# Expert 0 of a hybrid decoder layer: its rows picked by products with a slot matrix instead of gathered

## The reference

```
x = x + mix @ w_out                       # residual rows
h = rmsnorm(x, g_ffn)                     # x * 1/std(x) * g_ffn
logits = h @ w_router + b_router          # 512 x 32
top_val, top_idx = top_k(logits, 4); gates = softmax(top_val)
# for each expert e, on the rows of the tokens that chose it:
hu = h_rows @ w1[e] + b1[e]               # 1024 -> 2048
act = clamped_swiglu(hu)
y = act @ w2[e] + b2[e]                   # 1024 -> 1024
x = x + sum over the 4 experts of gate * y
out = rmsnorm(x, g_final)
```

## Time and profile before

| | us |
|---|---|
| median of 3 runs | 1236.43 (1236.21 to 1237.57) |
| the profiled execution | 1236.09 |
| its span, from first to last instruction | 1234.5 |
| PE busy, share of the span | 1158.3 (94%) |
| DVE busy | 306.6 (25%) |
| ACT busy | 191.7 (16%) |
| POOL busy | 174.2 (14%) |
| read from HBM | 442.60 MB |

### The profile page before, as it was taken

How to read it: one execution, slowest core, us unless ns; L and a number is a source line. 1 busy time by engine, 2 the same in 40 slices (tenths; PEclk the granted TensorE clock), 3 DMA queues, 4 the chain that set the end, 5 groups by cost and what they waited for, 6 DMA issues and landing times. The chain is left out here.

```text
span 1234.5 us, 16405 instructions
## 1 busy us (share of the span) xinstructions
PE 1158.3 (94%) x7022; PEld 481.7 (39%) x7022; DVE 306.6 (25%) x484; ACT 191.7 (16%) x378; POOL 174.2 (14%) x250
## 2 busy tenths in 40 slices
PE   5999998799999999999999999999999999999980
PEld 4777787223333333333333333333333333333330
DVE  4677756421111010101101010110101011010117
ACT  4453422011100101001100000110000010100002
POOL 6000100432101111110111111111111111111000
PEclk9999998799999999999999999999999999999996
DMA  9400675599999999999999999999999999999996
GB/s 336 148 1 3 224 309 214 173 368 404 426 426 425 426 429 423 426 425 429 424 425 425 427 427 424 427 426 427 423 426 427 426 425 427 426 425 427 427 383 235
DMA packets 51147, 454.39 MB, mean 368 GB/s; under 512 B 13044, under 2 KB 13316, under 8 KB 26400
## 3 DMA queue, kind: packets, MB, share of 16 engines
q1 hardware_dynamic: 42864, 434.16, 84.7%
q0 software_dynamic: 7632, 17.05, 3.6%
q10 hardware_dynamic: 576, 2.10, 0.4%
HBM read 442.60 MB, written 15.12 MB: 371 GB/s over the span
## 5 line engine op out<-in xcount | busy, mean ns | idle before, releaser
L846 PE MATMUL ps<-ring_a,blockT 128*64 128x512 f32 x1472 | 326.6, 597 | 8.5 <-DMA ring_a<-in_w 8.5
L1307 DVE TENSOR_SCALAR xnT<-ps 128x768 f32<-128x768 f32 (+1 forms) x32 | 26.9, 841 | 814.8 <-PE ps L853 516.1
L846 PEld LDWEIGHTS ps<-ring_a,blockT 128*64 128x64 f32 x1472 | 102.4, 137 | 218.5 <-issue 199.9
L872 PE MATMUL ps<-ring_a,actT 128*64 128x512 f32 x736 | 165.3, 596 | 0.8 <-DMA ring_a<-in_w 0.8
L846 PE MATMUL ps<-ring_b,blockT 128*64 128x512 f32 x448 | 99.5, 595 | 5.8 <-DMA ring_b<-in_w 5.8
L1594 ACT ACTIVATE blockT<-ps 128x512 f32<-128x512 f32 x30 | 17.9, 597 | 553.9 <-PE ps L793 553.9
L1780 POOL DMA_INDIRECT scores<-h_rows,slots x30 | 31.6, 1055 | 506.4 <-PE ps L793 505.5
L853 PE MATMUL ps<-ring_a,blockT 128*32 128x512 f32 x768 | 91.5, 615 | 0.0
L872 PEld LDWEIGHTS ps<-ring_a,actT 128*64 128x64 f32 x736 | 49.9, 136 | 93.6 <-issue 89.6
L1796 POOL DMA_INDIRECT expert_rows<-normed,slots x32 | 33.4, 1044 | 269.0 <-ACT normed L1623 268.7
L872 PE MATMUL ps<-ring_b,actT 128*64 128x512 f32 x288 | 64.7, 596 | 0.0
(11 more groups left out here) (300 smaller groups left out, 1069.0 us busy)
## 6 DMA issues: line engine op xcount, KB each, us to landing
ring_a<-in_w SPq DMA_DIRECT2D x144, 2048.0 KB, 30.0
ring_b<-in_w SPq DMA_DIRECT2D x48, 2048.0 KB, 31.6
ring<-in_w_in SPq DMA_DIRECT2D x12, 768.0 KB, 19.0
ring<-expert_rows SPq DMA_DIRECT2D x16, 512.0 KB, 14.0
X<-in_x SPq DMA_DIRECT2D x8, 512.0 KB, 6.5
ring<-in_w_out SPq DMA_DIRECT2D x8, 512.0 KB, 4.6
h_rows<-normed ACTq DMA_DIRECT2D x4, 512.0 KB, 3.6
out<-ring SPq DMA_DIRECT2D x4, 512.0 KB, 2.6
```

The source lines that it names most:

```text
L846: ins = mm(ps[half * HALF:(half + 1) * HALF, b, :], x_of(k)[0], ring(r)[:, 0, at + half * 512:at + (half + 1) * 512], start=False, stop=(k ...
L872: ins = mm(ps[half * HALF:(half + 1) * HALF, bank, :], actT[:, s % 2 * W2_K + j, s // 2 * HALF:(s // 2 + 1) * HALF], ring(r)[:, 0, j * D + ...
L1307: v.tensor_scalar(width(glu_c, big), width(ps_glu, big), LIMIT, None, ALU.min).then_inc(glu_ready, 1)
```

## The change

1. **Rows of expert 0.** They are no longer gathered. `place` makes, instead of expert 0's `pick`, a float32 matrix `sel_x` (128 tokens x 96 slots) for each tile, which holds 1/std of the token where the token takes the slot, and zero elsewhere. PE multiplies it by the residual rows (`select_x`: 8 products for each tile, summed over the four tiles in PSUM banks 1 and 6), and the result is the transposed rows of expert 0. ACT scales four blocks by `gain_pair` (4 instructions of 128x96), DVE the other four (1 of 128x384). `fetch(0)` and `turn_block(0)` go; the token sums are made for expert 1 alone.
2. **Last tile.** `turn_h2(3)` writes banks 2 and 3 and no longer waits for the copies of tile 2. The ranks of tile 3 get a bank of their own, `place(2, 4)` becomes `place(2, 3)` and `place(3, 4)`. On DVE `second_norm(3)` stands behind `turned_h2(3)`, on ACT `store_h2(3)` stands behind `turned_h2(3)`.
3. **Groups of two.** `w1_product` of the static experts runs groups of two blocks k.
4. **Loads.** `load_first(10)` waits for the four stores of the normed rows, `load_first(12)` for the rows of expert 1, which is the first gather now. One small parameter load (`gain_pair`) is added at the start.

```diff
+SELECT_BANKS = (1, 6)
+RANK_BANKS = (7, 7, 7, 0)
+TURN_BANKS = (4, 4, 4, 2)
...
             sp.wait_ge(oproj_done, 2 * TB)
-            load_first(4, 10)
-            sp.wait_ge(rows_in, fetches(0))
+            load_first(4)
+            sp.wait_ge(h2_stored, 16 * TB)
+            load_first(10)
+            sp.wait_ge(rows_in, fetches(1))
             load_first(12)
...
                 if t == 2:
-                    pe.wait_ge(pick_ready, 2 * t)
-                own = ps[:, 7, t * E:(t + 1) * E]
+                    pe.wait_ge(sel_ready_x, t)
+                if t == 3:
+                    pe.wait_ge(chosen_ready, TB)
+                own = ps[:, RANK_BANKS[t], t * E:(t + 1) * E]
...
+            def select_x(t):
+
+                if t == 0:
+                    pe.wait_ge(negtop_ready, TB - 1)
+                pe.wait_ge(sel_ready_x, t + 1)
+                for k in range(KT):
+                    rows = X[:, t, :].rearrange("p (s q j) -> p s j q", j=2, q=P)[:, k // 2, k % 2, :]
+                    ins = mm(ps[:, SELECT_BANKS[k // 4], k % 4 * MANY:(k % 4 + 1) * MANY], rows, sel_x[:, t, :],
+                             start=(t == 0 and k % 4 == 0), stop=(t == TB - 1 and k % 4 == 3))
+                if t == TB - 1:
+                    ins.then_inc(rows_turned, 1)
...
             turn_h2(2)
-            router(2)
             rank(0)
             rank(1)
             turn_h2(3)
+            router(2)
             router(3)
+            select_x(0)
             rank(2)
+            select_x(1)
             rank(3)
-
-            pe.wait_ge(pick_ready, 2 * TB)
-            for e in range(2):
+            select_x(2)
+            select_x(3)
+
+            pe.wait_ge(pick_ready, TB)
+            for e in range(1, 2):
...
                 w1_product(BIG[i], parity, lambda k: (w1_slot(i, k) % RING, *arrived[w1_slot(i, k)]),
-                           x_of_lines if i < STATIC else x_of_parts)
+                           *((x_of_lines, GROUP // 2) if i < STATIC else (x_of_parts,)))
...
             pe.wait_ge(biases_ready, 2)
-            turn_block(0)
             expert_blocks(compute)
...
                 for t in range(first, end):
-                    for e in range(2):
-                        v.tensor_scalar(pick[:, e, t, :], iota_r[:, :], own_rank[:, t, e:e + 1], None, ALU.is_equal).then_inc(pick_ready, 1)
+                    v.tensor_scalar(sel_x[:, t, :], iota_r[:, 0:MANY], own_rank[:, t, 0:1], stat[:, H_R + t:H_R + t + 1], ALU.is_equal, ALU.mult).then_inc(sel_ready_x, 1)
+                for t in range(first, end):
+                    v.tensor_scalar(pick[:, 1, t, :], iota_r[:, :], own_rank[:, t, 1:2], None, ALU.is_equal).then_inc(pick_ready, 1)
...
             select(2)
             select(3)
-            place(2, 4)
+            place(2, 3)
+            place(3, 4)
...
             dve.wait_ge(tok_summed, 1)
-            v.tensor_scalar(tok_static[:, :], ps[:, 5, 0:2], 16384.0, None, ALU.add).then_inc(tok_ready, 1)
-            then(v.tensor_copy(ranks[:, :, :].rearrange("p t e -> p (t e)"), ps[:, 7, 0:TB * E]))
+            v.tensor_scalar(tok_static[:, 1:2], ps[:, 5, 1:2], 16384.0, None, ALU.add).then_inc(tok_ready, 1)
+            dve.wait_ge(rows_turned, 1)
+            v.tensor_tensor(rowsT[:, 4:8, :], ps[:, SELECT_BANKS[1], 0:4 * MANY].rearrange("p (k t) -> p k t", k=4),
+                            gain_pair[:, 4:8].unsqueeze(2).to_broadcast([P, 4, MANY]), ALU.mult).then_inc(rows_ready, 1)
+            v.tensor_copy(ranks[:, 0:3, :].rearrange("p t e -> p (t e)"), ps[:, 7, 0:3 * E])
+            then(v.tensor_copy(ranks[:, 3, :], ps[:, 0, 3 * E:4 * E]))
...
-            fetch(0)
-            pool.wait_ge(rows_turned, 1)
             fetch(1)
```

More of the change, by code:

```diff
@@ L145, in layer_kernel @@
         gain_col = sb("gain_col", [P, KT])
+        gain_pair = sb("gain_pair", [P, KT])
         conv_wc = sb("conv_wc", [P, CONV_K, CT])
@@ L340, in fetches @@
         def fetches(upto):
-            return 16 * sum(2 if BIG[i] and i >= STATIC else 1 for i in range(upto + 1))
+            return 16 * sum(2 if BIG[i] and i >= STATIC else 1 for i in range(1, upto + 1))
         def scatters(parity, upto):
@@ L710, in turn_h2 @@
                     pe.wait_ge(gstd_ready, 1)
-                else:
+                elif t < TB - 1:
                     pe.wait_ge(h2T_a, t)
                     pe.wait_ge(h2T_b, t)
-                turn_rows(X[:, t, :], 4).then_inc(h2_turned, 1)
+                turn_rows(X[:, t, :], TURN_BANKS[t]).then_inc(h2_turned, 1)
             def router(t):
@@ L808, in turn_block @@
                     pe.wait_ge(rows_ready, 2)
-                elif i:
+                else:
                     pe.wait_ge(actT_ready, 2 * (i - 1))
@@ L828, in quarter_cols, with w1_product @@
                 return cols[:, :, q // 2, :, q % 2 * W2_K:(q % 2 + 1) * W2_K]
-            def w1_product(big, parity, slot, x_of):
+            def w1_product(big, parity, slot, x_of, group=GROUP):
                 for b, at in ((B_GLU, 0), (B_LIN, FF)):
@@ L839, in w1_product @@
                        start=True, stop=False, tile_position=(0, q * QUARTER))
-                for k0 in range(0, KT, GROUP):
-                    for k in range(k0, k0 + GROUP):
+                for k0 in range(0, KT, group):
+                    for k in range(k0, k0 + group):
                         r, done, value = slot(k)
@@ L849, in w1_product @@
                                     ins.then_inc(slot_used, 3)
-                    for k in range(k0, k0 + GROUP if big else k0):
+                    for k in range(k0, k0 + group if big else k0):
                         w = ring(slot(k)[0])[:, 0, :]
@@ L1179, in place @@
                 then(v.scalar_tensor_tensor(out=own_rank[:, tiles, :], in0=chosen[:, tiles, 0:2], scalar=-1024.0,
[L1180 removed]
+                                            in1=ps[:, RANK_BANKS[first], 0:TB * E].rearrange("p (t e) -> p t e", t=TB)[:, tiles, 0:2],
                                             op0=ALU.mult, op1=ALU.add))
                 for t in range(first, end):
[L1183 to L1184 removed]
+                    v.tensor_scalar(sel_x[:, t, :], iota_r[:, 0:MANY], own_rank[:, t, 0:1], stat[:, H_R + t:H_R + t + 1], ALU.is_equal, ALU.mult).then_inc(sel_ready_x, 1)
+                for t in range(first, end):
+                    v.tensor_scalar(pick[:, 1, t, :], iota_r[:, :], own_rank[:, t, 1:2], None, ALU.is_equal).then_inc(pick_ready, 1)
             residual(0, 0)
@@ L1585, in _ @@
             squares_h2(3)
+            turned_h2(3)
             store_h2(3)
-            turned_h2(3)
             for t in range(TB):
@@ L1600, in turned_rows @@
                 act.wait_ge(rows_turned, i + 1)
-                if isinstance(i, int) and i < STATIC:
+                if isinstance(i, int) and i == 0:
+                    for k in range(4):
+                        ins = a.activation(rowsT[:, k, :], ps[:, SELECT_BANKS[0], k * MANY:(k + 1) * MANY], ACT.Copy, scale=gain_pair[:, k:k + 1])
+                    ins.then_inc(rows_ready, 1)
+                elif isinstance(i, int) and i < STATIC:
                     for b in range(2):
```

14 lines of the change are left out of this document (8 added, 6 removed).

## The result

| | before | changed |
|---|---|---|
| median, us | 1236.43 | 1242.53 |
| lowest to highest, us | 1233.49 to 1237.84 | 1240.05 to 1248.16 |
| runs | 7 | 7 |
| profiled execution: time, span, us | 1236.09, 1234.5 | 1248.16, 1246.6 |

The ratio is 1.0056, 95% interval 1.0041 to 1.0072: slower by 6 us. On another chip, where the kernel before had 1234.80, the changed kernel gave 1.0051 (1.0033 to 1.0070). The profiled execution of the changed kernel is the slowest of its seven, so its moves of 10 to 12 us are larger than the usual one.

What follows compares the result with a forecast made beforehand. The weight-load stream from about 300 us bounds the kernel; its start follows expert 2's rows. List path 4.9 - 0.8 = +4.1 us beat PE's +3.6, giving 1240.2 profiled, 1240.5 median; range 1234.5 to 1245.

Steps and rivals of the forecast that it cites:

- The bound: From about 300 us the unbroken stream of weight loads sets the end; only when it begins can change.
- the anchor: PE's transposes of expert 2's rows at 276.78 us; moving them moves the load of 283.72 and the end one for one.
- Path (b): List path to the anchor: last list step, 16 stores, read-back, expert 2's gather; forecast +4.1 us and late last.
- The main term of the sum: Token numbers 4.2 us later, at 220.8 instead of 216.58, with half clock through the logits and part of the sets.
- my rival of a clock that stays at 2.4 GHz: From the last tile through the sets: token numbers at 216.7, +0.1 us; time 1236.4, same; chance 0.18.
- my own list: Signs against the prediction, including clock 1.00 through the sets or a set over 2.3 us at full clock.
- slack: Room of the list's path ahead of expert 2's transposes: taken as 0.8 us, bounds 0 and 1.3.
- full-clock case: Tile 3's logits take 1.94 us at full clock and end at 208.6 instead of 212.49.
- half-clock one: Tile 3's logits take 3.59 us at half clock and end at 210.3 instead of 212.49; the case taken.
- path (a): PE's path to the anchor: sorting, expert 0's first product, experts 0 and 1; forecast 2.6 + 1.0 = +3.6 us.
- DVE's steps: Behind the token numbers: the 128x384 multiplication out of PSUM, 0.55 us, and a second copy, 0.13, delay sorting and list.
- POOL's stores and gathers are taken unchanged: In the sum for path (b), the list's transfers add nothing; the range allowed -1 to +2 us for gather or read-back.

Runs made afterwards that it cites:

- e5: The changed kernel itself, timed and traced again on another chip: 1240.98 us, ratio 1.0051 to the kernel before.
- e6: Changed kernel with token sums and counts ahead of all four sets, which stand between the sorting's products, all scalings on ACT: 1242.02 us, ratio 1.0059 to before.
- e8: Changed kernel with the first set of eight select products issued three times: 1246.48 us, ratio 1.0097 to the kernel before.
- e2: Kernel before with groups of two in the static experts alone: 1241.46 us, ratio 0.9992 to the kernel before.
- e7: Kernel before with the last tile's part and groups of two, without the picked rows of expert 0: 1235.86 us, ratio 1.0015 to the kernel before.
- e3: Changed kernel with groups of four in the static experts, as before: 1241.94 us, ratio 1.0003 to the kernel before.
- e10: Changed kernel with eight memsets on POOL, 3 us in all, ahead of the list's stores: 1246.58 us, ratio 1.0039 to the kernel before.
- e12: The kernel before against itself, unchanged, for its trace on that chip: 1240.70 us, ratio 0.9993.
- e4: Kernel before with eight small fills on POOL, about 3 us, ahead of the list's 16 stores: 1243.77 us, ratio 1.0010 to the kernel before.
- e9: Changed kernel with groups of four, second set behind the counts, third and fourth behind the sorting's last products, scalings on ACT: 1245.20 us, ratio 1.0011 to before.

## Why the prediction was right, point by point

**The bound and the anchor: right.** The stream from 300 us is unchanged, and the end followed the load behind expert 2's rows (+11.9 for +12.3). The other traces agree. Beside the first trace of the kernel before, that load is 4.0 us later in e5, 10.2 in e6 and 13.5 in e8, and the span is 3.7, 10.0 and 13.2 us longer. The rest keep within 1.0 us, but for e2 and e7, with groups of two and no sets, which end 2.4 and 1.3 us sooner than their load says. Path (b) was last, as forecast: shown by the waits for the gather of 4.32, 3.48, 10.32 and 9.67 us in the traces of the changed kernel, e5, e6 and e8, all on chips that don't stall.

**The main term of the sum: true of the slowest execution only.** Times in us behind the start of tile 2's transposes take out what differs between executions ahead of the change:

| | before | changed, profiled | e5 |
|---|---|---|---|
| end of tile 3's logits | 10.5 | 6.4 | 6.4 |
| token numbers | 14.6 | 19.0 | 14.4 |
| last list step | 28.7 | 33.7 | 29.1 |
| gather of expert 2 landed | 73.9 | 83.3 | 77.7 |
| PE at expert 2's rows | 74.8 | 83.3 | 77.7 |
| the load behind them | 81.8 | 92.8 | 87.6 |

I had the token numbers 4.2 us later, by a clock at 1.2 GHz through the logits and part of the sets. In the profiled execution they are 4.4 later. In e5 they are 0.2 us earlier, since the logits and all four sets ran at 2.4 GHz; e3 and e10, with the same instructions up to there, have 14.4 too. So in three of four traces my rival of a clock that stays at 2.4 GHz held through the sets, by my own list a sign that the prediction is wrong, and its price for the token numbers, +0.1, was right. Its time was not: 1236.4, where e5's median is still 0.5% above before. Both sums leave out the same two terms, below. In e5 they are the loss: 0.4 at the list step + 3.4 of transfers - 0.9 of slack + 2.9 of clock = 5.8 us at the load, for medians 6.2 us apart. (In e12, e2 and e4, which have the instructions of the kernel before up to there, the list step stands at 28.3, 26.7 and 26.7, so 0.4 could be up to 2.4.)

**Part 2: the end of tile 3's logits came out by luck.** They ended at 209.62 against a forecast of 210.3 (212.49 before), but at full clock. Behind tile 2's transposes that is 6.4 us, which is my full-clock case (6.6) and not the half-clock one (8.3) that I took; the number fits because this execution reached tile 2 1.3 us late. The clock fell 0.5 us later, at 210.11, early in the first set.

**Groups of two: +1.0 forecast, +1.1 found on PE.** The stretch from expert 0's first ring product to the turn of its activation, as a window of the kernel before and then of e6:

```profile
226.98:274.86 47.88, 46.51 (x277) 13.84 (x273) 8.13 (x16) 3.00 (x4) 21.07 (x27) 0.97 0.77 287
```
```profile
226.58:273.90 47.32, 45.95 (x276) 12.75 (x273) 8.96 (x18) 3.00 (x4) 18.79 (x22) 1.00 0.88 301
```

e6 has it all at full clock, 47.3. Before, 3.33 us of the 47.88 ran at half clock, up to the rise at 230.31; work that fills them takes 1.67 at full clock, so 46.2. The same sum gives 47.3 for the changed kernel, for e5 and for e7. That is 1.1 us on path (a). Where the list is last it doesn't reach the end, and e2's time doesn't show it either.

**Part 1, the sets' own price: 10% too small.** A set took 2.0 us at full clock (3.99 for two) and 3.71 at half (the second in the changed kernel), against my 1.8 and 3.5. In the profiled execution I had let the clock rise 4.9 us behind 210.2; it took 10.2, from 210.11 to 220.35, and the token numbers came at 222.22 instead of 220.8. Next to e7, which has the logits' gain without the sets, the sets cost the sums 3.1 us in e5.

**DVE's steps: right.** Token numbers to end of sorting, 5.92 before, 6.56 after: +0.64 for a forecast of 0.68.

**The term that failed: "POOL's stores and gathers are taken unchanged".** They took 4.3 us longer in the changed kernel and 4.1 longer in e5 than in e7. Expert 2's gather went out at 276.89 where I had written 272.3; my range had up to 2 us for this, my sum nothing. Part 1 brings PE's products forward against the list: expert 0's first ring product stands 6.2 us ahead of the last list step in the changed kernel and in e5, 3.7 before and 2.4 in e7, so the loads that it releases run beside more of the stores. The windows of before and of the changed kernel, from the list step to the end of the stores, from there to the read-back, and from the read-back to the gather's issue, show the DMA engines busier in the first and the last:

```profile
230.64:251.93 21.29, 20.38 (x128) 6.14 (x124) 1.75 (x4) 0.87 (x2) 15.62 (x16) 1.00 0.64 214
258.99:267.37 8.38, 8.38 (x56) 2.33 (x54) 0.20 (x1) 0.00 (x0) 4.31 (x11) 1.00 0.81 295
```
```profile
236.92:258.20 21.28, 19.91 (x128) 5.67 (x122) 3.02 (x5) 2.84 (x4) 15.60 (x16) 0.99 0.89 268
267.47:276.89 9.42, 9.42 (x60) 2.44 (x58) 0.20 (x1) 0.00 (x0) 4.30 (x11) 1.00 0.98 397
```

The middle window speaks against it (share 0.99 and 7.1 us before, 0.91 and 9.3 us in the changed kernel). Over all traces it speaks for it again. In e2, e3, e4 and e10 the DMA engines are all but idle (0.01 to 0.03) between the last store and the read-back, and the read-back begins 2.4 to 3.5 us behind that store's issue. In the other ten, with shares of 0.70 to 1.02, it takes 6.2 to 10.2. But the head start of the products doesn't order the whole of it: in e6 it is 4.8 us, less than in e5, and the transfers took 53.7 us; e8 has e5's 6.2 and took 52.7. That the loads slow the list's transfers is therefore argued and not shown. I ran nothing that held the loads alone, and the cause stays open.

**A term that was not there: the clock at expert 2.** During each wait of 3 to 10 us for the gather the clock fell to 1.2 GHz, and the work up to the load behind it grew from 6.9 us to 9.5 (changed), 9.9 (e5), 8.8 (e6) and 9.1 (e8). So lateness of the list costs more than itself.

I forecast 4.1 at the anchor. The terms that the traces give are 6.3 + 4.3 - 0.9 + 2.6 for the profiled pair and 0.4 + 3.4 - 0.9 + 2.9 for e5 against before; the median moved 6.1. The direction and the late path were forecast for a reason that holds: the sets and DVE's work stand on the list's chain. That the time came within 2 us of the forecast is in part luck. In three of four traces the clock term that made up nearly all of my 4.1 was not there, and in e5 two terms that I had left out stood in its place. Of the seven executions behind the median only the slowest has a trace, so how they divide between the two cases is not known.

## What to carry to other kernels

Ask of each added product which chain it stands in, and whether another engine waits behind it in PE's stream for something small. Here 8 us of products at full clock saved 2.6 us between the end of sorting and the first product (2.8 before, 0.2 after) and stood in front of a token sum that a 60 us chain of list, stores, read-back and gather hung on. Where two paths meet within 1 us, a gain on one alone is worth at most that and a loss on the other counts nearly in full, and the transfers of the late path must be priced anew against the loads that now run beside them. Moving a block of work "off the sums" is no cure if it then stands in front of the next wait of the same chain.

## What the runs showed of the hardware that I had not expected

- The clock doesn't follow the work alone. After the same short wait (1.37 us for DVE ahead of expert 1's first product) it fell to 1.2 GHz in the changed kernel, e5 and e7, for some 3.4 us each, and stayed at 2.4 in e6, e8 and the kernel before. It cost 1.7 us each time: the first sixteen products behind it took 5.33 to 5.35 us instead of 3.65.
- It also fell amid unbroken work: PE was busy for 3.70 of 3.70 us from 206.40 to 210.10, the clock then fell, and PE stayed busy for all of the 10.20 us at 0.50, with float32 products of 32 and 96 columns. The Trainium skill, in "TensorE: Matmul & The Clock Gate", section "HAM oscillation — how this bites in real kernels", ties the fall to idle gaps; this row speaks against that as the only cause, while the falls during the waits for the gather agree with it.
- Float32 products of 96 columns against a 128x128 block take nearly as long as those of 32: 0.125 us an instruction (3.99 for 32) and 0.114 (3.66 for 32) at full clock, 0.23 and 0.22 at half. PEld was as busy as PE (10.18 of 10.20 us), from which I take it that the weight loads set the pace.
- An indirect store of one column of the list took a median of 6.9 us from issue to landing in one kernel and 9.3 in the other.
- On two of four chips PE paused 3 to 9 us for no recorded reason in the first static expert or right behind it, and the kernel before took 1242.7 instead of 1234.8 to 1236.4. In e9 the stall began near 241 us while the DMA engines were all but idle, so traffic of the weights' loads didn't start it there:

```profile
235.00:241.00 6.00, 5.67 (x40) 1.66 (x41) 0.00 (x0) 0.00 (x0) 4.78 (x5) 1.00 0.04 4
241.00:247.00 6.00, 3.08 (x8) 0.68 (x8) 0.00 (x0) 0.00 (x0) 3.91 (x5) 1.00 0.32 44
```

What its cause is stays open.
